# Both mixers' gate projections: high and low weight parts in one tile, two matmuls per slice instead of three

## The reference

```python
# fox: 16 heads, one forget gate each
proj = h @ w_in                         # 1024 x (3*1024 + 16)
q, k, v, f_logit = jnp.split(proj, [D_MODEL, 2 * D_MODEL, 3 * D_MODEL], axis=-1)
log_f = jax.nn.log_sigmoid((f_logit + b_f).astype(jnp.float32))
c = jnp.cumsum(log_f, axis=1).transpose(0, 2, 1)
...
logits = logits + cqb[..., :, None] - c[:, :, None, :]

# GLA: rank-16 gate
q, k, v, z_lr, r = jnp.split(proj, splits, axis=-1)
g = jax.nn.log_sigmoid((z_lr @ w_gate_up + b_gate).astype(jnp.float32)) / GLA_GATE_TAU
bc = jnp.cumsum(to_chunks(g, DK), axis=3)
```

## Time and profile before

| | |
|---|---|
| median of three executions | 1302.3 us |
| the profiled execution, own time | 1300.34 us |
| span in its trace, first to last instruction | 1298.6 us |
| mean granted TensorE clock, share of full speed | 0.991 |
| PE busy | 1254.0 us, 97% of the span |
| DVE busy | 647.5 us, 50% |
| ACT busy | 451.3 us, 35% |

### The profile page before, as it was taken

How to read it: one execution, slowest core, us unless ns; L and a number is a source line. 1 busy time by engine, 2 the same in 40 slices (tenths; PEclk the granted TensorE clock), 3 DMA queues, 4 the chain that set the end, 5 groups by cost and what they waited for, 6 DMA issues and landing times.

```text
span 1298.6 us, 15771 instructions
## 1 busy us (share of the span) xinstructions
PE 1254.0 (97%) x6133; PEld 1032.5 (80%) x6133; DVE 647.5 (50%) x886; ACT 451.3 (35%) x660; POOL 42.2 (3%) x86
## 2 busy tenths in 40 slices
PE   6999999999999999999988999998999999999997
PEld 4777777678888888888867898896888888888885
DVE  5645455444543434434447878886354343443432
ACT  6444344333422313313235334433252232231321
POOL 3000000000000000000011001000000000000000
PEclk9999999999999999999998999998999999999998
DMA  8111221212332323322211131231232233232001
GB/s 263 50 49 48 65 80 65 65 40 90 97 97 97 98 97 97 97 97 65 81 54 49 50 97 65 66 128 33 97 114 98 98 97 97 97 97 97 32 0 65
DMA packets 99701, 106.19 MB, mean 82 GB/s; under 512 B 4129, under 2 KB 78017, under 8 KB 99666
## 3 DMA queue, kind: packets, MB, share of 16 engines
q1 hardware_dynamic: 96880, 103.82, 25.0%
q10 hardware_dynamic: 2786, 1.89, 0.5%
HBM read 103.60 MB, written 2.10 MB: 81 GB/s over the span
## 4 chain that ended last, share of the span: by engine, by line
PE 84%; DVE 8%; issue 3%; ACT 3%; DMA 1%; POOL 0%; DVEq 0%; SPq 0%; ACTq 0%; POOLq 0%
PE bank L658 13%; PE bank L662 12%; PE bank L661 12%; PE bank L669 12%; PE bank L672 12%; PE bank L673 12%; PE bank L842 3%; PE bank L816 2%; PE bank L830 2%; DVE silu L1245 1%; PE bank L924 1%; DVE mx L1115 1%; DVE probs L1126 1%; ACT w_hi L440 1%; DMA w_stage<-in_fox_w_in_dram 1%
## 5 line engine op out<-in xcount | busy, mean ns | idle before, releaser
L999 DVE TENSOR_TENSOR w_lo<-w_stage,w_hi 128x2048 fp32r<-128x2048 f32 x104 | 229.6, 2209 | 241.8 <-ACT w_hi L440 241.7
L658 PE MATMUL bank<-hT_lo,w_hi 128*128 128x512 f32 x768 | 303.0, 395 | 1.8 <-DVE hT_lo L1018 1.0
L661 PE MATMUL bank<-hT_hi,w_hi 128*128 128x512 f32 x768 | 299.9, 391 | 0.0
L662 PE MATMUL bank<-hT_hi,w_lo 128*128 128x512 f32 x768 | 299.9, 390 | 0.0
L440 ACT ACTIVATE w_hi<-w_stage 128x2048 fp32r<-128x2048 f32 x104 | 191.8, 1847 | 290.2 <-PE bank L669 234.4
L673 PE MATMUL bank<-w_hi,u_lo 128*128 128x512 f32 x512 | 199.3, 389 | 0.0
L672 PE MATMUL bank<-w_hi,u_hi 128*128 128x512 f32 x512 | 199.3, 389 | 0.0
L669 PE MATMUL bank<-w_lo,u_hi 128*128 128x512 f32 x512 | 199.3, 389 | 0.0
L658 PEld LDWEIGHTS bank<-hT_lo,w_hi 128*128 128x128 f32 x768 | 144.7, 188 | 33.4 <-issue 1.9
L662 PEld LDWEIGHTS bank<-hT_hi,w_lo 128*128 128x128 f32 x768 | 144.6, 188 | 30.3
L661 PEld LDWEIGHTS bank<-hT_hi,w_hi 128*128 128x128 f32 x768 | 144.7, 188 | 29.0
(11 more groups left out here) (175 smaller groups left out, 1215.5 us busy)
## 6 DMA issues: line engine op xcount, KB each, us to landing
w_stage<-in_mlp_w_up_dram SPq DMA_DIRECT2D x32, 1024.0 KB, 5.1
w_stage<-in_mlp_w_down_dram SPq DMA_DIRECT2D x32, 1024.0 KB, 4.9
w_stage<-in_fox_w_in_dram SPq DMA_DIRECT2D x24, 512.0 KB, 4.6
w_stage<-in_gla_w_in_dram SPq DMA_DIRECT2D x8, 1024.0 KB, 5.0
w_stage<-in_gla_w_in_dram SPq DMA_DIRECT2D x8, 512.0 KB, 3.6
w_stage<-in_gla_w_out_dram SPq DMA_DIRECT2D x4, 1024.0 KB, 4.9
w_stage<-in_fox_w_out_dram SPq DMA_DIRECT2D x3, 1024.0 KB, 5.0
out_dram<-hn SPq DMA_DIRECT2D x4, 512.0 KB, 2.6
```

The source lines that it names most:

```text
L658: a = pe.matmul(out, w[0][:, k, :], x[1][:, k, :], start=(k == 0), stop=False)
L661: pe.matmul(out, w[0][:, k, :], x[0][:, k, :], start=False, stop=False)
L662: a = pe.matmul(out, w[1][:, k, :], x[0][:, k, :], start=False, stop=(k == KT - 1))
L999: dve.tensor_tensor(w_lo[:, slot, 0:n], w_stage[:, slot, 0:n], fp(w_hi[:, slot, 0:n]), ALU.subtract).then_inc(w_lo_made, 1)
```

## The change

Both gates' weights lie in one tile `gates_split` of 64 columns per slice: fox high, GLA high, fox residual, GLA residual, 16 columns each. A stationary block of 48 columns from column 0 (fox) or 16 (GLA) holds the high part in its first 16 columns and the residual of the same gate in its last 16; the middle 16 belong to the other gate and what they give is not used. One matmul of it by `hT_hi` gives both hi x hi (bank rows 0 to 15) and lo x hi (rows 32 to 47). A second matmul, 16 columns by `hT_lo`, adds hi x lo to rows 0 to 15. A tile is 16 matmuls. Rows 32 to 47 are added to rows 0 to 15 by VectorE: for f with a copy and an addition into `fg`, ahead of ScalarE's absolute value; for z with one addition into `zT`, behind ScalarE's copy.

```diff
-        gate_hi = sb("gate_hi", [P, 2, KT, RANK], F32R)
-        gate_lo = sb("gate_lo", [P, 2, KT, RANK], F32R)
+        gates_split = sb("gates_split", [P, KT, 4 * RANK], F32R)
+        gate_hi, gate_lo = (gates_split[:, :, j * LO_ROW:(j + 1) * LO_ROW].rearrange("p k (g n) -> p g k n", g=2)
+                            for j in range(2))
...   # ScalarE
-            act.wait_ge(f_done, 1)
+            act.wait_ge(f_summed, 1)
-            act.activation(fg[:, 0, :], bank[1][0:FOX_H, :], ACT.Abs, bias=bf_col[:, 0:1]).then_inc(f_abs, 1)
+            act.activation(fg[:, 0, :], fg[:, 1, :], ACT.Abs, bias=bf_col[:, 0:1]).then_inc(f_abs, 1)
...   # TensorE
+            def gate_tile(b, which, before):
+                def hi_and_lo(k):
+                    return pe.matmul(bank[b][0:GATE_ROWS, :], gates_split[:, k, which * RANK:which * RANK + GATE_ROWS],
+                                     hT_hi[:, k, :], start=(k == 0), stop=(k == KT - 1))
+                def hi_only(k):
+                    pe.matmul(bank[b][0:RANK, :], gates_split[:, k, which * RANK:(which + 1) * RANK], hT_lo[:, k, :],
+                              start=False, stop=False)
+                before(0)
+                hi_and_lo(0)
+                for k in range(1, KT):
+                    before(k)
+                    hi_only(k - 1)
+                    if k < KT - 1:
+                        hi_and_lo(k)
+                hi_only(KT - 1)
+                a = hi_and_lo(KT - 1)
+                return a
...
-            tile(bank[1][0:FOX_H, :], (gate_hi[:, 0], gate_lo[:, 0]), hT,
-                 lambda k: pe.wait_ge(gate_lo_made, 1) if k == 0 else None).then_inc(f_done, 1)
+            gate_tile(1, 0, ready_gate).then_inc(f_done, 1)
...
-            tile(bank[0][0:RANK, :], (gate_hi[:, 1], gate_lo[:, 1]), hT, ready(2)).then_inc(z_done, 1)
+            gate_tile(0, 1, ready(2)).then_inc(z_done, 1)
-            pe.wait_ge(z_copied, 1)
+            pe.wait_ge(z_summed, 1)
...   # VectorE
+            dve.wait_ge(f_done, 1)
+            mine.then(dve.tensor_copy(fg[:, 0, :], bank[1][0:FOX_H, :]))
+            dve.tensor_tensor(fg[:, 1, :], bank[1][LO_ROW:GATE_ROWS, :], fg[:, 0, :], ALU.add).then_inc(f_summed, 1)
             dve.wait_ge(f_abs, 1)
-            mine.then(dve.tensor_scalar(fg[:, 1, :], bank[1][0:FOX_H, :], bf_col[:, 0:1], 0.0, ALU.add, ALU.min))
+            mine.then(dve.tensor_scalar(fg[:, 1, :], fg[:, 1, :], bf_col[:, 0:1], 0.0, ALU.add, ALU.min))
...
+            dve.wait_ge(z_copied, 1)
+            dve.tensor_tensor(zT[0:RANK, :], bank[0][LO_ROW:GATE_ROWS, :], zT[0:RANK, :], ALU.add).then_inc(z_summed, 1)
             dve.wait_ge(gla_filled, 5)
             dve.tensor_tensor(xor[:], xor[:], other[:], ALU.bitwise_xor).then_inc(xor_made, 1)
```

More of the change, by code:

```diff
@@ L21 @@
 EPS = 1e-6
+LO_ROW, GATE_ROWS = 32, 48
 DFF = 4 * D
@@ L203, in fox_gla_trunk @@
         w_hi_made, w_lo_made, w_begun = sem("w_hi_made"), sem("w_lo_made"), sem("w_begun")
-        gate_hi_made, gate_lo_made = sem("gate_hi_made"), sem("gate_lo_made")
+        gate_hi_made, gate_lo_made, f_summed = sem("gate_hi_made"), sem("gate_lo_made"), sem("f_summed")
         pool_step, ident_made, fox_consts_made, qz_zeroed = (
@@ L226, in fox_gla_trunk @@
         o_done, o_hi_made, o_lo_made = sem("o_done"), sem("o_hi_made"), sem("o_lo_made")
-        z_done, z_copied = sem("z_done"), sem("z_copied")
+        z_done, z_copied, z_summed = sem("z_done"), sem("z_copied"), sem("z_summed")
         gq_done, gk_done, gq_copied, gk_copied = (
@@ L502, in _ @@
             act.wait_ge(gate_w_loaded, 32)
-            act.activation(gate_hi[:], gate_w[:], ACT.Copy).then_inc(gate_hi_made, 1)
+            act.activation(gate_hi, gate_w[:], ACT.Copy).then_inc(gate_hi_made, 1)
             split_hi(0, 0, 1, UNIT // 2)
@@ L676, in _, with ready_gate @@
             hT = (hT_hi, hT_lo)
+            def ready_gate(k):
+                if k == 0:
+                    pe.wait_ge(gate_lo_made, 1)
+            def gate_tile(b, which, before):
[15 more added lines that the diff above has]
+                return a
             def unit(i, per, c, shape=None, first=0):
@@ L1081, in _ @@
             dve.wait_ge(gate_hi_made, 1)
-            dve.tensor_tensor(gate_lo[:], gate_w[:], fp(gate_hi[:]), ALU.subtract).then_inc(gate_lo_made, 1)
+            dve.tensor_tensor(gate_lo, gate_w[:], fp(gate_hi), ALU.subtract).then_inc(gate_lo_made, 1)
             split_lo(0, 0, 1, UNIT // 2)
```

## The result

Over 20 executions of each, the changed kernel took 1303.23 us (1299.7 to 1307.02), the kernel before 1300.73 us (1299.29 to 1302.47). The ratio is 1.0018, 95% interval 1.001 to 1.0025: slower by 2.3 us, where 0.3 us faster was forecast. (The forecast's 1302.0 us was counted from 1302.3 us, the median of three executions; over 20 the kernel before is at 1300.73, so the same forecast is 1300.4 us on this scale.) The profiled execution took 1304.46 us, with a span of 1302.7 us and a mean clock of 0.987 in place of 0.991.

A forecast was written before the change was run, and what follows sets the result against it. TensorE is 97% busy, but at both starts chains of small ScalarE and VectorE instructions were taken as already as long as its work. Terms -0.69 + 0.38 = -0.3 us gave 1302.0 us, 8-in-10 range 1300.3 to 1303.9.

The forecast's parts named there:

- The two terms: Gain at the fox start, -0.69 us, and loss at the GLA start, +0.38 us; together -0.3 us.
- Fox start: Eight f matmuls fewer, two VectorE instructions more: v copy starts 0.69 us earlier, between -1.2 and -0.3 us.
- GLA start: Eight z matmuls gain only 0.25 us, VectorE's sum lengthens the chain: L902 0.38 us later.
- the term is +0.38 us: At the GLA start, the z tile's gain and VectorE's sum net +0.38 us; +0.1 or +0.6 with other sum durations.
- rival 2: TensorE's longer pauses bring half clock, up to 1.7 us per stretch, 1305.4 us with both; 13% one, 7% both.
- a half-clock row in 680 to 687: Around L902 at the GLA start, listed among the profile signs that would show the forecast wrong; no size given.
- both its forms: One more half-clock stretch on the path, 1303.7 us, 13%; two, 1305.4 us and above, 7%.
- Rival 1: Matmuls come off whole at both the fox and GLA starts: 3.7 us, time 1298.6 us; 3%.
- Rival 4: New VectorE instructions hold up ScalarE beyond 0.6 us of slack, making the k copy late: 1304 us; 5%.
- Rival 3: A half-clock stretch now on the path, as at 707.88, falls elsewhere with shifted times: 1300.3 us; 10%.

The follow-up runs named there:

- e4: Changed kernel plus six matmuls with unused results behind the z tile, ahead of the wait for VectorE's sum; 1299.98 us, ratio 0.9999 to the kernel before.
- e9: e5 plus six matmuls with unused results behind the z tile, ahead of the wait; 1300.22 us, ratio 0.9992 to the kernel before.
- e5: Changed kernel with z's 24 matmuls restored and, for the sum, a VectorE maximum that changes nothing; 1302.37 us, ratio 1.0011 to the kernel before.
- e6: Changed kernel with 16 z matmuls that leave out high weights by low activations, and no sum; 1300.43 us, ratio 1.0003 to the kernel before.
- e7: e1 with VectorE's v copy moved ahead of the weight split that stood before it; 1298.22 us, ratio 0.9982 to the kernel before.
- e2: Changed kernel with the f tile and its chain put back, so only z is changed; 1304.29 us, ratio 1.0034 to the kernel before.
- e8: Changed kernel with z's sum made by the gate matmuls, the gate weights standing twice in 48 rows; 1300.21 us, ratio 0.9994 to the kernel before.
- t4: Third trace of the kernel before, nothing changed; single time 1301.41 us.
- e1: Changed kernel with the z tile and its chain put back, so only f is changed; 1299.99 us, ratio 0.9998 to the kernel before.
- e10: e4 with VectorE's v copy moved ahead of the weight split; 1299.55 us, ratio 0.9987 to the kernel before.
- t1: Second trace of the changed kernel, nothing changed; single time 1304.11 us.

## Why the prediction was wrong

**The two terms were right.** Fox start: -0.69 forecast, -0.70 measured. The new VectorE instructions took 0.67 and 0.68 us (0.69 taken); they started some 0.1 us before the shown end of the weight splits (27.52, where 24.18 + 3.43 = 27.61); the v copy (40.60) came on the heels of the split, and the pause is 1.93 us. Where I had the absolute value shorten by 0.05 us for reading SBUF, it took 0.72, 0.04 longer. VectorE's next link, freed of the bank, took 0.48 in place of 0.74, and made no difference, as VectorE waits for ScalarE's logarithm behind it. The wider stationary block cost nothing, as taken: 16 matmuls of 48 and 16 columns in turn started (27.08 - 23.58) / 15 = 0.233 us apart. GLA start: +0.38 forecast, +0.47 measured. The last slice of `hT_lo` was ready at 674.04 + 5.36 = 679.40, the last matmul started 0.52 us behind it, as forecast, and the sum took 0.68 us. The 0.09 us lie in the hand-over from VectorE to TensorE, 0.15 us (681.72 to 681.87), where I had set 0.05 by the transposes; L902 waits about as long behind ScalarE (0.14), which suggests that this matmul starts later than a transpose, whoever releases it; no run tests that.

**The step that failed** is "the term is +0.38 us", taken as the whole cost of the longer wait: its price in clock stood in the sum at nothing, on the ground that the pauses of 0.8 us brought no half clock at once, though this pause was to grow to 1.45 us. The prediction knew this price only as rival 2, and its own sign for it, a half-clock row in 680 to 687, came. The gate matmuls took 3.4, 2.6 and 3.3 us more than at full clock in the three traces of the changed kernel, and 0, 0 and 2.1 in those of the kernel before. In sum, +2.3 us measured less -0.23 by the two terms leaves 2.5 us for the clock, and that is what e4 gives back (2.5) and e9 against e5 (2.5). How these 2.5 us of the median divide between the gate matmuls, the scan and the transposes ahead of z (see Open) three traces can't tell. That 1303.23 us lies within the stated range is luck: the range was set around a time before that was 1.6 us too high.

**Rival 2** had the right mechanism, and at the GLA start the right place and size (up to 1.7 us for 3.4 us of half clock; here 7.1 us at half). On the fox start it did not come in the three traces of the changed kernel, with their pause of 1.9 us ahead of the transposes; of the seven other traces with this pause, those of e4 and e6 had a stretch of 3.4 us near 41.5. It was wrong on the odds, 20% for both its forms. I reasoned from where the clock had fallen and not from what would meet it: the trace of before had a fall 0.7 us behind the last gate matmul, which could have been read as a narrow escape. The Trainium skill ("TensorE: Matmul & The Clock Gate", section "Why this matters for your kernels") warns of long idle gaps between bursts of matmuls. The waits here, of 1.5 us, are well short of those that it names, and by e4, e5 and e9 they cost clock all the same; here the measurement decides.

**The other rivals.** Rival 1 (all 16 matmuls) was out as reckoned, but e7 shows that at the fox start only one weight split on VectorE stood between 0.7 and 1.84 us. Rival 4 did not happen: the k copy was still started by TensorE. Rival 3 can't be told from the mixture: the stretch near 233 is missing from the first trace of the changed kernel and stands in the other two.

**Open.** All three traces of the changed kernel have half clock over the transposes ahead of the z tile too (671 to 675 in the first), none of the three before. But e2, e4 and e8 have none either, and e5 and e9 have it, so I can't tie it to a part of the change. From the start of the last MLP matmul to that of the z tile it is 8.5 us without it, and 8.6, 9.2 and 9.8 us in the three traces of the changed kernel; so it costs 0.1 to 1.3 us. The half-clock stretch at the gates, where there is one, starts between 681.8 and 688.2 us in all traces; what ties it to that place wasn't tried.

## What to carry to other kernels

Ahead of a chain of small instructions, matmuls saved on an engine that must wait for the chain are only turned into waiting; first look which engine's order holds up the next hand-over (here one weight split: with it moved the eight matmuls are worth 1.8 us, without 0.7). A wait lengthened by one instruction of 0.7 us can cost 2.5 us beyond its own length, where small matmuls behind it stand on the path and the clock is near a fall; a fall close behind them in the trace of before may be the warning (one case, read afterwards). Where a short wait can't be avoided, a few matmuls into a free bank kept the clock up over the matmuls behind it in all five traces that have them, but putting the sum into a matmul that is there anyway (e8) needs neither.

## What the runs showed of the hardware

Half clock over tiles ahead of a pause is paid for out of the pause: with 5.7 us of it over the q and k tiles (t4) in place of 3.4 (before) the pause at the scan was 1.6 us in place of 2.8, and the scan began no later behind the gate matmuls (21.25 us in both). The length of the pause alone doesn't say whether the clock falls: behind pauses of 1.6 (t4, e1) and of 2.9 to 3.1 us (e7, e9, e10) the scan took 178.3 us, at full clock, and behind 2.1 (t1, e2) and 2.8 us (before) 179.8 to 179.9, at half clock first. With stationary blocks of 16, 48 and 128 columns, matmuls of 512 columns start 0.23 us apart. A float32 matmul of 512 columns with 48 rows on the contracted side takes what one with 17 takes: 3.67 us for the eight in both cases (e8 and before). An addition or copy of 16x512 out of a bank on VectorE took 0.67 to 0.68 us, as much as one of 128x512 (0.69).
